# One of four weight-block sums of every turn by seven products moves from VectorE to an adding transfer on the GpSimd queue

## The chip, the cores and the metric

The kernel runs on one core of a Trainium2 chip. The metric is the device time of one execution in microseconds (us), lower is better; three runs of the kernel before are given. A profile is one further execution, recorded by the hardware profiler.

## What is computed

Two transformer-like blocks over 256 tokens and 2048 features, all in float32. The first is a gated MLP with a spatial mixing, the second holds attention, an mLSTM and a gated convolutional MLP. Nearly all of the arithmetic is in products of the 256 tokens with large weight matrices:

```python
z = h @ w_in                                  # (256 x 2048) @ (2048 x 12288): u, v, gate
x = x + (y * jax.nn.silu(gate)) @ w_out       # (256 x 4096) @ (4096 x 2048)        phase out1
z = jnp.einsum('bsd,de->bse', h, w_in[l])     # 2048 -> 10256                        vv, side, gm
x = x + jnp.einsum('bsd,de->bse', merged, w_out[l])                               #  out2
u = causal_dwconv(jnp.einsum('bsd,df->bsf', h2, w_up[l]), conv_w[l], conv_b[l])   #  up
x = x + jnp.einsum('bsf,fd->bsd', jax.nn.silu(u_gate) * u_val, w_down[l])         #  down
```

## The kernel before

**The stream of weights.** All weights lie in HBM as chunks of 128 partitions x 1024 float32 (512 KB, 256 rows by 512 columns of a matrix), in the order in which they are used. Every weight is used once. TensorE multiplies in a reduced float32 format (`fp32r`), so each chunk is split in two: ScalarE copies it into `w_hi` in that format (`high_of_chunk`, line 1014, "hi" below), VectorE computes `w_lo` = chunk - `w_hi` (`low_of_chunk`, line 1432, "lo" below), and TensorE makes three matmuls of every tile: hi by hi, lo by hi and hi by lo. `w_hi` and `w_lo` are rings of four slots. ScalarE starts the hi of item n once TensorE is through with item n - 4 (`mm_done`), VectorE follows (`hi_ready`), and TensorE waits for `lo_ready`. Every engine takes its work in one fixed order, that of the list `ITEMS`.

**Items.** An ordinary item is one chunk of the stream (12 matmuls, 16 in phase up). In the phases v, out1, gm0, gm1, out2 and down some of the work is done in *turns by seven products*: a turn there covers a 2 x 2 set of matrix blocks B11, B12, B22, B21 (each a chunk of its own, with a buffer of its own), and the eight block products of the two token tiles and two column halves are made out of seven, by sums of row tiles and sums of weight blocks (the Winograd form of Strassen's scheme). A product is an item of 6 matmuls. There are 21 such turns (`QUADS`): 5 in v, 4 in out1, 3 in gm0 and gm1, 2 in out2, 7 in down. Their products stand between the chunks C0 to C3 of an ordinary turn; "a chunk item" is one of those:

```python
MIXED = (1, "C0", 5, 7, "C1", 6, 3, "C2", 4, 2, "C3")
MIXED_LATE = ("C0", 1, "C1", 5, 7, "C2", 6, 3, "C3", 4, 2)      # gm1 and out2
```

**The sums of weight blocks.** Product 1 multiplies B11, product 3 B22, product 2 B21. The other four multiply sums, which VectorE makes in place (`block_sum`, line 1437), called *T1* to *T4* here in the order in which they are made: T1 = B12 - B11 (into B11's buffer, for product 5), T3 = B22 - B12 (into B12's buffer, for product 7), T2 = B22 - T1 (for product 6), T4 = B21 - T2 (for product 4). T1 is made after the lo of product 1, T3 after the lo of the item behind product 1, T2 after the lo of product 5. ScalarE's hi of product 7 waits for T3 by the semaphore `block_sums`.

**Queues.** All weights are loaded by SyncE's queue (`raw` chunks four ahead into a ring, line 504, and the blocks, line 491), each after the lo of the item that used its buffer. GpSimd (POOL) has 14 small operations (`rstd`, line 2042, a power) and nothing else.

**Order of back-to-back turns.** In `WIDE_STEPS` a pair such as `(2, 4)` is one turn by products mixed with one ordinary turn. Of the 21 turns by products 9 follow directly on another of them in the same phase, in `MIXED` order; 9 stand in `MIXED` order behind ordinary chunk items; 3 are in `MIXED_LATE` order.

```python
"down": (((3, None), (4, None), (8, None), (9, None), (5, 0), (6, 1), (7, 2), (10, None)),
         ((3, 0), (7, None), (4, 1), (5, 2), (8, 6), (9, None), (10, None))),
```

Of the kernel before, what the change touches and what calls it, by code (L numbers as in the profile page):

```python
# [13 lines left out]
M_HEADS = 4  # L14
# [161 lines left out]
def quad_of(item):  # L176

    return QUADS.index((item.phase, item.group, item.turn))
# [84 lines left out]
def build(nc, x, x_tokens, stream, w_s, params, gain_rows, final_rows, gate_w, identity, consts, out):  # L263
# [208 lines left out]
    with block:  # L472
# [520 lines left out]
        def _(act):  # L993
# [3 lines left out]
            def high_of_chunk(n):  # L997

                item = ITEMS[n]
                if item.product:  # L1000
                    b, uses = PRODUCT_OF[item.product], quad_of(item)
                    of = wide[item.phase].blocks[buffer_of(uses, b)]
                    if item.product in (1, 3, 2):
                        act.wait_ge(block_full[b], 16 * (uses + 1))
                    else:
                        act.wait_ge(sem["block_sums"], 4 * uses + {5: 1, 7: 2, 6: 3, 4: 4}[item.product])
                else:
                    c = CHUNK_COUNT[n]
                    of = raw[:, c % RING, :]
                    act.wait_ge(raw_full[c % RING], 16 * (c // RING + 1))  # L1010
                if n >= RING:

                    act.wait_ge(mm_done, n - RING + 1)
                activation(w_hi[:, n % RING, :], of[:], ACT.Copy).then_inc(hi_ready, 1)  # L1014
# [405 lines left out]
        def _(dve):  # L1420
# [13 lines left out]

            def block_sum(item, to, a, b):
                to, a, b = (wide[item.phase].blocks[buffer_of(quad_of(item), k)] for k in (to, a, b))
                v.tensor_tensor(to[:], a[:], b[:], ALU.subtract).then_inc(sem["block_sums"], 1)

            def block_sums(n):

                item, before = ITEMS[n], ITEMS[n - 1]
                if item.product == 1:
                    uses = quad_of(item) + 1
                    dve.wait_ge(block_full[B11], 16 * uses)
                    dve.wait_ge(block_full[B12], 16 * uses)
                    dve.wait_ge(lo_ready, n + 1)
                    block_sum(item, B11, B12, B11)
                elif before.product == 1:
                    uses = quad_of(before) + 1
                    dve.wait_ge(block_full[B22], 16 * uses)  # L1450
                    dve.wait_ge(sem["block_sums"], 4 * uses - 3)
                    block_sum(before, B12, B22, B12)
                elif item.product == 5:
                    dve.wait_ge(lo_ready, n + 1)
                    block_sum(item, B11, B22, B11)
                elif item.product == 6:
                    dve.wait_ge(block_full[B21], 16 * (quad_of(item) + 1))
                    dve.wait_ge(lo_ready, n + 1)
                    block_sum(item, B11, B21, B11)
# [53 lines left out]
            def sums_of_rows(phase, n, a_hi, a_lo):  # L1513

                if n in SUMS_AT[phase]:
                    i = SUMS_AT[phase].index(n)
                    at_i = slice(4 * SUM_TURNS[phase][i], 4 * SUM_TURNS[phase][i] + 4)
                    rows, sums = wide[phase].rows, wide[phase].sums
                    link(v.tensor_tensor(rows[:], a_hi[:, at_i, :].bitcast(F32), a_lo[:, at_i, :].bitcast(F32), ALU.add))
                    a11, a21 = rows[:, 0:2, 0:P], rows[:, 0:2, P:S]  # L1520
                    a12, a22 = rows[:, 2:4, 0:P], rows[:, 2:4, P:S]
                    v.tensor_tensor(sums[:, 2], a11, a21, ALU.subtract)
                    link(v.tensor_tensor(sums[:, 0], a21, a22, ALU.add))
                    link(v.tensor_tensor(sums[:, 1], sums[:, 0], a11, ALU.subtract))
                    v.tensor_tensor(sums[:, 3], a12, sums[:, 1], ALU.subtract).then_inc(sem["sums_ready"], 1)

            def sums_low(phase, n):
# [5 lines left out]
            def own_products(phase, n):  # L1533


                p1, u_a, u_b = wide[phase].p1, wide[phase].u_a, wide[phase].u_b
                for name, g in GROUPS_BY_PRODUCTS:
                    if name != phase:
                        continue
                    after = n - product_item(phase, g, last_by_products(phase, g), 6)  # L1540
                    if after == 0:
                        dve.wait_ge(sem["p1_ready"], own_ahead(phase, g) + 1)
                        dve.wait_ge(mm_done, n + 1)
                        link(v.tensor_tensor(u_a[:], XS[:, 2, :], p1[:], ALU.add))
                    if after == 2:
                        link(v.tensor_tensor(u_b[:], XS[:, 3, :], u_a[:], ALU.add))
                    if after == 4:
                        link(v.tensor_tensor(u_a[:], XS[:, 1, :], u_a[:], ALU.add))
# [8 lines left out]
            def v_result(q):  # L1557

                half = q % 2
                dve.wait_ge(mm_done, half_end("v", q // 2, half) + 1)  # L1560
                to = v_all[:, :, col_block(q)]
                by_t = ((v_wide.p1, v_wide.u_b), (v_wide.u_a, v_wide.u_d))[half]
                for t in range(2):
                    ins = v.tensor_tensor(to[:, t, :], GG[:, 2 * half + t, :], by_t[t][:], ALU.add)  # L1564
                ins.then_inc(group_read[half], 1)

            for n in range(items_of("v")):
# [92 lines left out]
            def add_products(phase, n, to):  # L1660

                p1, u_a, u_b = wide[phase].p1, wide[phase].u_a, wide[phase].u_b
                for g in range(2):
                    n0, n1 = col_block(2 * g), col_block(2 * g + 1)
                    at_6 = product_item(phase, g, last_by_products(phase, g), 6)
                    after = n - at_6
                    if after == 0:
                        dve.wait_ge(sem["p1_ready"], own_ahead(phase, g) + 1)
                        dve.wait_ge(mm_done, at_6 + 1)
                        link(v.tensor_tensor(u_a[:], XS[:, 2, :], p1[:], ALU.add))  # L1670
                        v.tensor_tensor(to[:, 0, n0], to[:, 0, n0], p1[:], ALU.add)
                    if after == 1:
                        link(v.tensor_tensor(u_b[:], XS[:, 3, :], u_a[:], ALU.add))
                        v.tensor_tensor(to[:, 1, n0], to[:, 1, n0], u_b[:], ALU.add)
                    if after == 2:
                        link(v.tensor_tensor(u_a[:], XS[:, 1, :], u_a[:], ALU.add))
                        v.tensor_tensor(to[:, 0, n1], to[:, 0, n1], u_a[:], ALU.add)
                    if after == 3:
                        link(v.tensor_tensor(u_b[:], XS[:, 1, :], u_b[:], ALU.add))
                        link(v.tensor_tensor(to[:, 1, n1], to[:, 1, n1], u_b[:], ALU.add))  # L1680
                        dve.sem_inc(sem["own_read"], 1)

            out1_second = product_item("out1", 1, 4, 1) - FIRST_ITEM["out1"] - 8
# [184 lines left out]
            def gate_m_result(gm, h):  # L1868

                dve.wait_ge(mm_done, half_end(gm, 0, h) + 1)  # L1870
                by_t = ((gm_wide.p1, gm_wide.u_b), (gm_wide.u_a, gm_wide.u_d))[h]
                for t in range(2):
                    ins = v.tensor_tensor(gate_m[h][:, t, :], GG[:, 2 * h + t, :], by_t[t][:], ALU.add)
                ins.then_inc(group_read[h], 1)

            def a_projected(p, h):
# [159 lines left out]
        @block.gpsimd  # L2036
        def _(pool):
            p = nc.gpsimd

            def rstd(to, of, count, value, after):  # L2040
                pool.wait_ge(sem[count], value)
                p.tensor_tensor(to, of, minus_half[:, 0:of.shape[1]], ALU.pow).then_inc(sem[after], 1)

            pool.wait_ge(sem["minus_half_ready"], 1)
            rstd(n_rstd[:, 0:2], n_ms[:, 0:2], "ms_ready", 1, "rstd_ready")
            rstd(v_stat[:, 4:6], v_stat[:, 2:4], "v_ms_ready", 1, "v_rstd_ready")
            rstd(n_rstd[:, 0:2], n_ms[:, 0:2], "ms_ready", 2, "rstd_ready")
            rstd(n_rstd[:, 2:4], n_ms[:, 2:4], "ms_ready", 3, "rstd_ready")
            for n in range(4):
                rstd(q_rstd[:], q_ms[:], "q_ms_ready", n + 1, "q_rstd_ready")  # L2050
            for m in range(M_HEADS):
                rstd(m_rstd[:], m_ms[:], "m_ms_ready", m + 1, "m_rstd_ready")
            rstd(n_rstd[:, 0:2], n_ms[:, 0:2], "ms_ready", 4, "rstd_ready")


def chunks_of(w):
# [75 lines left out]
```

## Time and profile before

| | |
|---|---|
| time, median of 3 runs | 2098.22 us (2098.14 to 2098.47) |
| profiled execution, span | 2095.9 us |
| TensorE (PE) busy | 2089.8 us, 100% of the span, 10000 matmuls |
| VectorE (DVE) busy | 1506.6 us, 72% |
| ScalarE (ACT) busy | 1112.4 us, 53% |
| GpSimd (POOL) busy | 17.5 us, 1% |
| DMA queue of SyncE | 394.66 MB, 57.1% of the 16 DMA engines' span |

The time of a run stands 2.3 us above the span of the profiled execution. Times in the views are microseconds from the span's start. Matmuls are pipelined, so that one is recorded as 0.39 us long although the next starts 0.23 us after it.

### The profile page before, as it was taken

How to read it: one execution, taken by the hardware profiler on the slowest of the kernel's cores; microseconds unless marked ns; L12 is line 12 of the kernel's file. 1: busy time of each engine (PE TensorE's matmuls, PEld its weight loads, DVE VectorE, ACT ScalarE, POOL GpSimd, SP SyncE). 2: the span in 40 equal slices, each digit the busy share in tenths (PEclk: the TensorE clock that was granted, in tenths of full speed). 3: DMA queues.
4: the chain of work that ended last, by engine and by line, in shares of the span. 5: the costliest groups of instructions: out<-in, count | busy, mean ns of one | idle time of the engine just before them, and what ended most of it. 6: DMA issues, size and time to landing. Idle time of an engine off the chain costs nothing.

```text
span 2095.9 us, 25218 instructions
## 1 busy us (share of the span) xinstructions
PE 2089.8 (100%) x10000; PEld 1750.1 (84%) x10000; DVE 1506.6 (72%) x1702; ACT 1112.4 (53%) x1314; POOL 17.5 (1%) x17
## 2 busy tenths in 40 slices
PE   9999999999999999999999999999999999999999
PEld 7888888888888887888888888888888888888887
DVE  7987656655787754665669678867777777779986
ACT  6765444444456544555455454555555555555553
POOL 0000000000000000100000000000000000000000
PEclk9999999999999999999999999999999999999999
DMA  8665555555764555544465656556556566556663
GB/s 337 210 200 175 198 187 187 194 187 189 272 214 157 194 194 171 177 155 153 150 210 181 221 169 208 167 185 192 187 185 195 183 192 190 181 181 232 224 203 133
DMA packets 111957, 404.40 MB, mean 193 GB/s; under 512 B 12512, under 2 KB 13280, under 8 KB 111328
## 3 DMA queue, kind: packets, MB, share of 16 engines
q1 hardware_dynamic: 109440, 394.66, 57.1%
q10 hardware_dynamic: 2400, 8.14, 1.0%
q8 instruction: 79, 1.29, 0.3%
q14 instruction: 38, 0.31, 0.0%
HBM read 400.65 MB, written 2.10 MB: 192 GB/s over the span
## 4 chain that ended last, share of the span: by engine, by line
PE 96%; DVE 3%; ACT 1%; DMA 0%; issue 0%; ACTq 0%; DVEq 0%
PE g L556 37%; PE g L653 23%; PE xs L581 8%; PE g L581 8%; PE xs L676 5%; PE xs L585 4%; PE g L585 4%; PE g L680 4%; DVE w_lo L1432 1%; PE xs L604 1%; PE xs L713 1%; ACT w_hi L1014 0%; PE xs L833 0%; DMA xf<-in_x 0%; PE xs L830 0%
## 5 line engine op out<-in xcount | busy, mean ns | idle before, releaser
L1432 DVE TENSOR_TENSOR w_lo<-raw,w_hi 128x1024 fp32r<-128x1024 f32 x659 | 803.4, 1223 | 492.6 <-ACT w_hi L1014 486.9
L1014 ACT ACTIVATE w_hi<-raw 128x1024 fp32r<-128x1024 f32 x659 | 697.4, 1059 | 756.6 <-PE g L556 411.7
L556 PE MATMUL g<-w_hi,mid_both 128*128 128x512 f32 x1024 | 326.7, 394 | 0.0
L556 PE MATMUL g<-w_hi,in_both 128*128 128x512 f32 x1024 | 318.8, 390 | 0.1
L556 PEld LDWEIGHTS g<-w_hi,in_both 128*128 128x128 f32 x1024 | 192.2, 188 | 40.3 <-DVE v_all L1564 0.5
L556 PEld LDWEIGHTS g<-w_hi,mid_both 128*128 128x128 f32 x1024 | 192.3, 188 | 39.6
L556 PE MATMUL g<-w_lo,mid_both 128*128 128x512 f32 x512 | 199.4, 389 | 0.0
L556 PE MATMUL g<-w_lo,in_both 128*128 128x512 f32 x512 | 199.2, 389 | 0.0
L581 PE MATMUL g<-mlp_both,w_hi 128*128 128x512 f32 x704 | 176.8, 393 | 0.0
L581 PE MATMUL xs<-mlp_both,w_hi 128*128 128x512 f32 x704 | 176.3, 392 | 0.0
L581 PEld LDWEIGHTS g<-mlp_both,w_hi 128*128 128x128 f32 x704 | 126.5, 189 | 22.8
L581 PEld LDWEIGHTS xs<-mlp_both,w_hi 128*128 128x128 f32 x704 | 126.6, 189 | 22.6
L653 PE MATMUL g<-w_hi,in_both 128*128 128x512 f32 x352 | 112.6, 390 | 1.3 <-DVE w_lo L1500 1.0
L556 PEld LDWEIGHTS g<-w_lo,in_both 128*128 128x128 f32 x512 | 96.1, 188 | 19.7
L556 PEld LDWEIGHTS g<-w_lo,mid_both 128*128 128x128 f32 x512 | 96.3, 188 | 19.1
L585 PEld LDWEIGHTS g<-mlp_both,w_lo 128*128 128x128 f32 x704 | 96.2, 190 | 7.0
L585 PEld LDWEIGHTS xs<-mlp_both,w_lo 128*128 128x128 f32 x704 | 96.0, 190 | 6.9
L585 PE MATMUL g<-mlp_both,w_lo 128*128 128x256 f32 x704 | 98.3, 282 | 0.0
L585 PE MATMUL xs<-mlp_both,w_lo 128*128 128x256 f32 x704 | 98.2, 282 | 0.0
L653 PE MATMUL g<-w_hi,f_hi 128*128 128x512 f32 x240 | 93.7, 390 | 0.2
L653 PE MATMUL g<-w_hi,f_lo 128*128 128x512 f32 x240 | 93.4, 389 | 0.0
L653 PE MATMUL g<-w_lo,f_hi 128*128 128x512 f32 x240 | 93.4, 389 | 0.0
(404 smaller groups left out, 3044.3 us busy)
## 6 DMA issues: line engine op xcount, KB each, us to landing
raw<-in_stream SPq DMA_DIRECT2D x659, 512.0 KB, 3.5
d_block<-in_stream SPq DMA_DIRECT2D x28, 512.0 KB, 4.6
o_block<-in_stream SPq DMA_DIRECT2D x24, 512.0 KB, 4.7
v_block<-in_stream SPq DMA_DIRECT2D x20, 512.0 KB, 4.4
gm_block<-in_stream SPq DMA_DIRECT2D x12, 512.0 KB, 5.1
x_first<-in_x_tokens ACTq DMA_DIRECT2D x2, 1024.0 KB, 6.8
gain_row<-in_gain_rows SPq DMA_DIRECT2D x8, 256.0 KB, 3.5
xt<-in_x_tokens ACTq DMA_DIRECT2D x1, 2048.0 KB, 8.0
```

What stands on the lines that cost most here:

```text
L556: ins = mm(G[buf][:, t, :], a[:, kt, at_t], w[:, slot, j * COLS:(j + 1) * COLS], start=(kt == 0 and n == 0), stop=(last and j == ROWS_PER_ ...
L581: mm(UP[buf][:, b, :, :], w_hi[:, slot, j * COLS + b * P:j * COLS + (b + 1) * P], a_both[:, :, kt, :], start=(kt == 0), stop=False, skip_g ...
L585: ins = mm(UP[buf][:, b, 0, :], w_lo[:, slot, j * COLS + b * P:j * COLS + (b + 1) * P], a_both[:, 0, kt, :], start=False, stop=(last and j ...
L604: ins = turn(TR[:, b, t * P:(t + 1) * P], of[:, t, b * P:(b + 1) * P], ident[:])
L653: ins = mm(GG[:, bank, :], a[:, kt, t * P:(t + 1) * P], w[:, slot, half_chunk(j)], start=n == 0 and opens(item, bank), stop=ended and n == ...
L676: ins = mm(XS[:, own[p], :], a, w[:, slot, half_chunk(j)], start=first and opens_own(item), stop=last and j == 1 and n == 2, skip_group_ch ...
L680: ins = mm(GG[:, RESULT_OF[p], :], a, w[:, slot, half_chunk(j)], start=first and opens(item, RESULT_OF[p]), stop=False, skip_group_check=True)
L713: ins = mm(SV[:, t, :], w[:, t, :], a[:, t, :], start=(n == 0), stop=(n == 2))
L1014: activation(w_hi[:, n % RING, :], of[:], ACT.Copy).then_inc(hi_ready, 1)
L1432: v.tensor_tensor(w_lo[:, n % RING, :], of, w_hi[:, n % RING, :].bitcast(F32), ALU.subtract).then_inc(lo_ready, 1)
```

## The change

T3 is no longer made on VectorE. GpSimd's queue issues a transfer, `add_block`, once per turn by products: it reads the chunk of B22 from HBM a second time and adds it to what lies in B12's buffer (`accum_op=ALU.add`). It waits for T1 (`block_sums` at 3q + 1 for the turn number q), because T1 reads the same buffer; ScalarE's hi of product 7 waits for its end (`block_added`). Since the transfer can only add, the signs of some blocks and of the sums of rows are turned: T1 = B12 + B11, T3 = B12 + B22, T2 = T1 + B22, T4 = T2 + B21, and the results of the second column half are subtracted where they were added. The `rstd` operations of GpSimd keep their order and are put between the transfers.

```diff
@@ high_of_chunk, ScalarE @@
                     if item.product in (1, 3, 2):
                         act.wait_ge(block_full[b], 16 * (uses + 1))
+                    elif item.product == 7:
+                        act.wait_ge(sem["block_added"], 16 * (uses + 1))
                     else:
-                        act.wait_ge(sem["block_sums"], 4 * uses + {5: 1, 7: 2, 6: 3, 4: 4}[item.product])
+                        act.wait_ge(sem["block_sums"], 3 * uses + {5: 1, 6: 2, 4: 3}[item.product])
@@ block_sum and block_sums, VectorE @@
             def block_sum(item, to, a, b):
                 to, a, b = (wide[item.phase].blocks[buffer_of(quad_of(item), k)] for k in (to, a, b))
-                v.tensor_tensor(to[:], a[:], b[:], ALU.subtract).then_inc(sem["block_sums"], 1)
+                v.tensor_tensor(to[:], a[:], b[:], ALU.add).then_inc(sem["block_sums"], 1)
 
             def block_sums(n):
 
-                item, before = ITEMS[n], ITEMS[n - 1]
+                item = ITEMS[n]
                 if item.product == 1:
                     uses = quad_of(item) + 1
                     dve.wait_ge(block_full[B11], 16 * uses)
                     dve.wait_ge(block_full[B12], 16 * uses)
                     dve.wait_ge(lo_ready, n + 1)
                     block_sum(item, B11, B12, B11)
-                elif before.product == 1:
-                    uses = quad_of(before) + 1
-                    dve.wait_ge(block_full[B22], 16 * uses)
-                    dve.wait_ge(sem["block_sums"], 4 * uses - 3)
-                    block_sum(before, B12, B22, B12)
                 elif item.product == 5:
+                    dve.wait_ge(block_full[B22], 16 * (quad_of(item) + 1))
                     dve.wait_ge(lo_ready, n + 1)
                     block_sum(item, B11, B22, B11)
@@ sums_of_rows, VectorE @@
                     v.tensor_tensor(sums[:, 2], a11, a21, ALU.subtract)
-                    link(v.tensor_tensor(sums[:, 0], a21, a22, ALU.add))
-                    link(v.tensor_tensor(sums[:, 1], sums[:, 0], a11, ALU.subtract))
+                    link(v.tensor_tensor(sums[:, 0], a22, a21, ALU.subtract))
+                    link(v.tensor_tensor(sums[:, 1], sums[:, 0], a11, ALU.add))
                     v.tensor_tensor(sums[:, 3], a12, sums[:, 1], ALU.subtract).then_inc(sem["sums_ready"], 1)
@@ add_products, VectorE (the same kind of edit in own_products, v_result, gate_m_result) @@
                     if after == 2:
                         link(v.tensor_tensor(u_a[:], XS[:, 1, :], u_a[:], ALU.add))
-                        v.tensor_tensor(to[:, 0, n1], to[:, 0, n1], u_a[:], ALU.add)
+                        v.tensor_tensor(to[:, 0, n1], to[:, 0, n1], u_a[:], ALU.subtract)
@@ GpSimd @@
+            def add_block(n):
+
+                item = ITEMS[n]
+                if item.product == 1:
+                    q = quad_of(item)
+                    pool.wait_ge(sem["block_sums"], 3 * q + 1)
+                    p.dma_start(wide[item.phase].blocks[buffer_of(q, B12)][:],
+                                stream[chunk_in_stream(item.phase, item.group, 1, 2 * item.turn + 1)],
+                                accum_op=ALU.add).then_inc(sem["block_added"], 16)
+
             pool.wait_ge(sem["minus_half_ready"], 1)
-            rstd(n_rstd[:, 0:2], n_ms[:, 0:2], "ms_ready", 1, "rstd_ready")
-            rstd(v_stat[:, 4:6], v_stat[:, 2:4], "v_ms_ready", 1, "v_rstd_ready")
-            rstd(n_rstd[:, 0:2], n_ms[:, 0:2], "ms_ready", 2, "rstd_ready")
-            rstd(n_rstd[:, 2:4], n_ms[:, 2:4], "ms_ready", 3, "rstd_ready")
-            for n in range(4):
-                rstd(q_rstd[:], q_ms[:], "q_ms_ready", n + 1, "q_rstd_ready")
-            for m in range(M_HEADS):
-                rstd(m_rstd[:], m_ms[:], "m_ms_ready", m + 1, "m_rstd_ready")
-            rstd(n_rstd[:, 0:2], n_ms[:, 0:2], "ms_ready", 4, "rstd_ready")
+            for n in range(1, FIRST_ITEM["end"]):
+                add_block(n)
+                if n == FIRST_ITEM["v"] + 18:
...
+                if n == FIRST_ITEM["up"]:
+                    rstd(n_rstd[:, 0:2], n_ms[:, 0:2], "ms_ready", 4, "rstd_ready")
```

VectorE in the second turn by products of phase down, before. `d_block_166` holds B11, `d_block_167` B12 and `d_block_165` B22:

```order
L1432 TENSOR_TENSOR w_lo<-d_block_166,w_hi 128x1024
L1437 TENSOR_TENSOR d_block_166<-d_block_167,d_block_166 128x1024
L1432 TENSOR_TENSOR w_lo<-raw,w_hi 128x1024
L1437 TENSOR_TENSOR d_block_167<-d_block_165,d_block_167 128x1024
L1432 TENSOR_TENSOR w_lo<-d_block_166,w_hi 128x1024
L1437 TENSOR_TENSOR d_block_166<-d_block_165,d_block_166 128x1024
L1432 TENSOR_TENSOR w_lo<-d_block_167,w_hi 128x1024
```

The same place after the change:

```order
L1434 TENSOR_TENSOR w_lo<-d_block_166,w_hi 128x1024
L1439 TENSOR_TENSOR d_block_166<-d_block_167,d_block_166 128x1024
L1434 TENSOR_TENSOR w_lo<-raw,w_hi 128x1024
L1434 TENSOR_TENSOR w_lo<-d_block_166,w_hi 128x1024
L1439 TENSOR_TENSOR d_block_166<-d_block_165,d_block_166 128x1024
L1434 TENSOR_TENSOR w_lo<-d_block_167,w_hi 128x1024
```

The fourth of the seven operations, T3, is gone, and all others keep their order.

ScalarE at the same place, with the semaphores that each instruction waits for, before:

```order
L1014 ACTIVATE w_hi<-d_block_166 128x1024 [waits mm_done,block_full0]
L1014 ACTIVATE w_hi<-raw 128x1024 [waits mm_done,raw_full0]
L1014 ACTIVATE w_hi<-d_block_166 128x1024 [waits mm_done,block_sums]
L1014 ACTIVATE w_hi<-d_block_167 128x1024 [waits mm_done,block_sums]
L1014 ACTIVATE w_hi<-raw 128x1024 [waits mm_done,raw_full1]
```

and after the change:

```order
L1016 ACTIVATE w_hi<-d_block_166 128x1024 [waits mm_done,block_full0]
L1016 ACTIVATE w_hi<-raw 128x1024 [waits mm_done,raw_full0]
L1016 ACTIVATE w_hi<-d_block_166 128x1024 [waits mm_done,block_sums]
L1016 ACTIVATE w_hi<-d_block_167 128x1024 [waits mm_done,block_added]
L1016 ACTIVATE w_hi<-raw 128x1024 [waits mm_done,raw_full1]
```

Nothing moved on ScalarE; the hi of product 7 (the fourth row) waits for the transfer. On TensorE the order of instructions is the same in both kernels.

## Rows read from the trace of the kernel before

**Rows 1.** The page, part 1: busy time, share, instructions of each engine.

```profile
PE 2089.8 (100%) x10000; PEld 1750.1 (84%) x10000; DVE 1506.6 (72%) x1702; ACT 1112.4 (53%) x1314; POOL 17.5 (1%) x17
```

**Rows 2.** Waits of TensorE over the whole span: in total, times, longest (us).

```profile
PE xs L609 <- DVE ones L1487: 1.1, 1, 1.1
PE g L653 <- DVE w_lo L1500: 1.0, 1, 1.0
PE g L653 <- DVE v_all L1564: 0.2, 1, 0.2
PE xs L780 <- DVE gw_both L1474: 0.2, 1, 0.2
```

**Rows 3.** The page, part 4: shares of the chain that ended last.

```profile
PE 96%; DVE 3%; ACT 1%; DMA 0%; issue 0%; ACTq 0%; DVEq 0%
```

**Rows 4.** Groups by line: the sums of blocks in down (xcount | busy us, mean ns).

```profile
L1437 DVE TENSOR_TENSOR d_block<-d_block,d_block 128x1024 f32<-128x1024 f32 x28 | 34.3, 1224 | 2.3 <-DVE w_lo L1432 0.5
```

**Rows 5.** Timeline of VectorE, second turn by products of down (start, us).

```profile
1922.20 1.23 DVE L1432 TENSOR_TENSOR w_lo<-d_block,w_hi 128x1024 fp32r<-128x1024 f32 x1 [1.49 <-ACT w_hi L1014]
1923.56 1.23 DVE L1437 TENSOR_TENSOR d_block<-d_block,d_block 128x1024 f32<-128x1024 f32 x1
1924.70 1.22 DVE L1432 TENSOR_TENSOR w_lo<-raw,w_hi 128x1024 fp32r<-128x1024 f32 x1
1925.84 1.22 DVE L1437 TENSOR_TENSOR d_block<-d_block,d_block 128x1024 f32<-128x1024 f32 x1
1926.97 1.22 DVE L1432 TENSOR_TENSOR w_lo<-d_block,w_hi 128x1024 fp32r<-128x1024 f32 x1
1928.23 1.23 DVE L1437 TENSOR_TENSOR d_block<-d_block,d_block 128x1024 f32<-128x1024 f32 x1
1929.37 1.22 DVE L1432 TENSOR_TENSOR w_lo<-d_block,w_hi 128x1024 fp32r<-128x1024 f32 x1
```

**Rows 6.** Timeline of ScalarE in the same stretch: hi of products 5 and 7.

```profile
1924.82 1.06 ACT L1014 ACTIVATE w_hi<-d_block 128x1024 fp32r<-128x1024 f32 x1 [1.29 <-DVE d_block L1437]
1927.09 1.06 ACT L1014 ACTIVATE w_hi<-d_block 128x1024 fp32r<-128x1024 f32 x1 [1.21 <-DVE d_block L1437]
```

**Rows 7.** Timeline of TensorE: first and last of the six matmuls of that product 7.

```profile
1931.73 0.39 PE L676 MATMUL xs<-w_hi,d_sums_hi 128*128 128x512 f32 x1
...
1932.87 0.39 PE L676 MATMUL xs<-w_hi,d_sums_lo 128*128 128x512 f32 x1
```

**Rows 8.** Timelines: T1 of the first turn in v, then its product 7.

```profile
48.02 1.23 DVE L1437 TENSOR_TENSOR v_block<-v_block,v_block 128x1024 f32<-128x1024 f32 x1
...
57.42 0.39 PE L676 MATMUL xs<-w_hi,v_sums_hi 128*128 128x512 f32 x1
```

**Rows 9.** Timelines: T1 of the fourth turn of down, then its product 7.

```profile
1972.64 1.23 DVE L1437 TENSOR_TENSOR d_block<-d_block,d_block 128x1024 f32<-128x1024 f32 x1
...
1983.41 0.39 PE L676 MATMUL xs<-w_hi,d_sums_hi 128*128 128x512 f32 x1
```

**Rows 10.** SyncE's DMA queue, issues (KB each, median us to landing), all blocks' landing.

```profile
q1 hardware_dynamic: 109440, 394.66, 57.1%
...
raw<-in_stream SPq DMA_DIRECT2D x659, 512.0 KB, 3.5
...
x_first<-in_x_tokens ACTq DMA_DIRECT2D x2, 1024.0 KB, 6.8
...
final_row<-in_final_rows ACTq DMA_DIRECT2D x1, 1024.0 KB, 12.1
...
DMA to landing us min/median/max: 3.0/4.7/9.4
```

**Rows 11.** Timeline: a wait of GpSimd for VectorE, and the operation before it.

```profile
55.16 0.16 DVE L1485 TENSOR_SCALAR n_ms<-n_sum 128x2 f32<-128x2 f32 x1
...
55.47 1.53 POOL L2042 TENSOR_TENSOR n_rstd<-n_ms,minus_half 128x2 f32<-128x2 f32 x1 [55.03 <-DVE n_ms L1485]
```

**Rows 12.** Timeline of SyncE's queue in the turn of rows 5.

```profile
1920.74 5.54 SPq L504 DMA_DIRECT2D raw<-in_stream  x2
```

More of the change, by code:

```diff
@@ L1543, in own_products @@
                         dve.wait_ge(mm_done, n + 1)
-                        link(v.tensor_tensor(u_a[:], XS[:, 2, :], p1[:], ALU.add))
+                        link(v.tensor_tensor(u_a[:], p1[:], XS[:, 2, :], ALU.subtract))
                     if after == 2:
@@ L1563, in v_result @@
                 for t in range(2):
-                    ins = v.tensor_tensor(to[:, t, :], GG[:, 2 * half + t, :], by_t[t][:], ALU.add)
+                    ins = v.tensor_tensor(to[:, t, :], GG[:, 2 * half + t, :], by_t[t][:], ALU.subtract if half else ALU.add)
                 ins.then_inc(group_read[half], 1)
@@ L1669, in add_products @@
                         dve.wait_ge(mm_done, at_6 + 1)
-                        link(v.tensor_tensor(u_a[:], XS[:, 2, :], p1[:], ALU.add))
+                        link(v.tensor_tensor(u_a[:], p1[:], XS[:, 2, :], ALU.subtract))
                         v.tensor_tensor(to[:, 0, n0], to[:, 0, n0], p1[:], ALU.add)
@@ L1676, in add_products @@
                         link(v.tensor_tensor(u_a[:], XS[:, 1, :], u_a[:], ALU.add))
-                        v.tensor_tensor(to[:, 0, n1], to[:, 0, n1], u_a[:], ALU.add)
+                        v.tensor_tensor(to[:, 0, n1], to[:, 0, n1], u_a[:], ALU.subtract)
                     if after == 3:
                         link(v.tensor_tensor(u_b[:], XS[:, 1, :], u_b[:], ALU.add))
-                        link(v.tensor_tensor(to[:, 1, n1], to[:, 1, n1], u_b[:], ALU.add))
+                        link(v.tensor_tensor(to[:, 1, n1], to[:, 1, n1], u_b[:], ALU.subtract))
                         dve.sem_inc(sem["own_read"], 1)
@@ L1872, in gate_m_result @@
                 for t in range(2):
-                    ins = v.tensor_tensor(gate_m[h][:, t, :], GG[:, 2 * h + t, :], by_t[t][:], ALU.add)
+                    ins = v.tensor_tensor(gate_m[h][:, t, :], GG[:, 2 * h + t, :], by_t[t][:], ALU.subtract if h else ALU.add)
                 ins.then_inc(group_read[h], 1)
@@ L2042, in rstd @@
                 p.tensor_tensor(to, of, minus_half[:, 0:of.shape[1]], ALU.pow).then_inc(sem[after], 1)
-            pool.wait_ge(sem["minus_half_ready"], 1)
-            rstd(n_rstd[:, 0:2], n_ms[:, 0:2], "ms_ready", 1, "rstd_ready")
-            rstd(v_stat[:, 4:6], v_stat[:, 2:4], "v_ms_ready", 1, "v_rstd_ready")
-            rstd(n_rstd[:, 0:2], n_ms[:, 0:2], "ms_ready", 2, "rstd_ready")
-            rstd(n_rstd[:, 2:4], n_ms[:, 2:4], "ms_ready", 3, "rstd_ready")
-            for n in range(4):
-                rstd(q_rstd[:], q_ms[:], "q_ms_ready", n + 1, "q_rstd_ready")
-            for m in range(M_HEADS):
-                rstd(m_rstd[:], m_ms[:], "m_ms_ready", m + 1, "m_rstd_ready")
-            rstd(n_rstd[:, 0:2], n_ms[:, 0:2], "ms_ready", 4, "rstd_ready")
+            def add_block(n):
[6 more added lines that the diff above has]
+                                accum_op=ALU.add).then_inc(sem["block_added"], 16)
+            pool.wait_ge(sem["minus_half_ready"], 1)
+            for n in range(1, FIRST_ITEM["end"]):
+                add_block(n)
+                if n == FIRST_ITEM["v"] + 18:
+                    rstd(n_rstd[:, 0:2], n_ms[:, 0:2], "ms_ready", 1, "rstd_ready")
+                if n == FIRST_ITEM["ug"]:
+                    rstd(v_stat[:, 4:6], v_stat[:, 2:4], "v_ms_ready", 1, "v_rstd_ready")
+                if n == FIRST_ITEM["vv"]:
+                    rstd(n_rstd[:, 0:2], n_ms[:, 0:2], "ms_ready", 2, "rstd_ready")
+                    rstd(n_rstd[:, 2:4], n_ms[:, 2:4], "ms_ready", 3, "rstd_ready")
+                if n == FIRST_ITEM["side"]:
+                    for k in range(4):
+                        rstd(q_rstd[:], q_ms[:], "q_ms_ready", k + 1, "q_rstd_ready")
+                    for m in range(M_HEADS):
+                        rstd(m_rstd[:], m_ms[:], "m_ms_ready", m + 1, "m_rstd_ready")
+                if n == FIRST_ITEM["up"]:
+                    rstd(n_rstd[:, 0:2], n_ms[:, 0:2], "ms_ready", 4, "rstd_ready")
 def chunks_of(w):
```

## The prediction

> **What bounds the kernel now.** I read the page first. TensorE is busy for 2089.8 of the 2095.9 us of the span [rows 1], and the chain that ended last runs through it for 96% [rows 3]. A matmul's recorded end is modelled, so a busy share alone could hide idle time; I therefore looked at TensorE's waits. There are four, 2.5 us in all, two of them before the first item [rows 2]. So in the steady state TensorE always finds its next operands. VectorE, at 72%, works ahead of it. What can change the time is only whether something comes to be late for TensorE.
>
> How far the others are ahead I read from the timeline of one turn by products in down, the second there. VectorE's lo of product 1 starts at 1922.20, T1 at 1923.56, so T1 ends at 1924.79; then come lo of the chunk, T3, lo of product 5, T2, and lo of product 7 from 1929.37 to 1930.59 [rows 5]. ScalarE waits for T1 before the hi of product 5 and for T3 before that of product 7 [rows 6]. TensorE starts product 7 at 1931.73 [rows 7]: lo of product 7 was there 1.14 us early. The reader is to see that T3 is a short link (ScalarE started 0.02 us after its end at 1927.07), and that the whole lead of the ring at this place is about one microsecond plus what VectorE would gain by a shorter list.
>
> **What it removes.** One of four sums in each of 21 turns. A sum takes 1224 ns [rows 4], so VectorE has 21 x 1.22 = 25.7 us less to do. None of it is on the path: TensorE waits for VectorE for 2.5 us in all, at places without a sum of blocks [rows 2]. The gain to the end is taken as 0 and can't be above 2.5 us. The row sums and the results keep their number of operations; only their signs change: 0. The wait for B22 goes from T3 to T2, one item later, which can only help.
>
> **What it adds.** In each turn, a chain in place of T3: T1 ends, GpSimd sees it and issues the transfer, the transfer reads B22 from HBM and adds it to B12's buffer, ScalarE sees its end and makes the hi of product 7. Queued behind that instruction on ScalarE are the hi of the chunk C1, of product 6 and so on, since ScalarE keeps its order; VectorE's lo of product 7 and all behind it wait for them, and TensorE waits for that lo.
>
> *How long may it take?* In the turn of rows 5 TensorE wants product 7 at 1931.73, its first weight load one matmul step (0.23 us) sooner, at 1931.50. Back from there: lo 1.22, hi 1.06, and about 0.15 for the two handings over, makes 2.43: ScalarE has to start by 1929.07, which is 4.3 us after the end of T1 [rows 5 to 7]. VectorE's own work doesn't come in between any more (lo of the chunk, lo of product 5 and T2 are three steps of 1.14 to 1.26, done by 1928.4). The 4.3 us hold for the 9 turns that follow directly on another one: the items ahead are then small, products 4 and 2 of the last turn among them. I count the first turn of gm0 with them, since VectorE comes to it late out of phase side: 10 turns. In the fourth turn of down, behind ordinary chunks, T1 ends at 1973.87 and product 7 starts at 1983.41 [rows 9]: less 0.23 and 2.43 that leaves 6.9. In the first turn of v it is 49.25 to 57.42 [rows 8], which leaves 5.5. By their timelines 4 turns lie between 5.5 and 6.9, and 7 (three of them in the late order) at 6.9 to 8.
>
> *How long does it take?* The trace has no transfer from GpSimd's queue and none that adds. Bounds: it can't be quicker than the quickest block load of the same 512 KB, 3.0 us, and for the other end I take the slowest 1024 KB load, 12.1 [rows 10]. An adding transfer has 512 KB to read in HBM and the 512 KB to which it adds; that is nearest to a load of 1024 KB, 6.8 us in this trace with the stream running beside it [rows 10]. It won't have the engines to itself here either: SyncE issues two raw loads in this stretch, the second when T3 used to start [rows 12]. GpSimd's start after VectorE's semaphore is 0.15 us (55.32 to 55.47) [rows 11]. I take 6.8 + 0.1 = 6.9 us from the end of T1 to the start of hi.
>
> *The sum.* TensorE's wait in a turn is what 6.9 goes beyond its allowance. Ten turns: 10 x (6.9 - 4.3) = 26. Four turns between: 1.4 in the first, half of that on average, 3. Seven turns: 0. Together 29 us of new waiting. I don't let one turn's wait spill into the next: after a late product 7, VectorE has the lo of 8 items and T4 to do, 9 x 1.14 = 10.3 us, while TensorE has 3 chunk items and 5 products, 3 x 2.72 + 5 x 1.36 = 15.0 us by its step of 0.23 (five steps from 1931.73 to 1932.87, so 1.36 for the six matmuls of a product and twice that for a chunk's twelve) [rows 7], so the lead is rebuilt before the next T1. Profiled execution: 2095.9 + 29 = 2125; the median of the runs stands 2.3 us above the span, so 2127.
>
> **A rule against this sum.** No row shows GpSimd's queue. The Trainium skill, "DMA: Bandwidth & Descriptors", section on the anatomy of one DMA, gives a GpSimd-issued transfer as about 2.0 us plus its bytes over 436 GB/s, which would be 3.2 us for 512 KB. "Collectives: The Full Stack", on the fold count, says that the adding costs nothing by itself but needs two reads, so counted as twice the bytes it would be 4.4 us. By that estimate nearly every turn would stay within its allowance, and the time would be about 2100; no run here shows it yet.
>
> **Rivals.**
> 1. *The transfer lands in time, no change.* Mechanism: the whole link takes under 4.7 us. Ten waits of up to 0.4 are then 4 us. For it: plain loads of this size land in 3.5 median, block loads in 4.7 [rows 10], and with the second read hidden under the first the link would be like one of them. Against: that is the price without adding and without GpSimd's issue, and the allowance is already used up by it. At 4.3 or less the time is 2098, at 4.7 it is 2102.
> 2. *The transfer is much slower*, as the 12.1 us row: then no turn is spared. The allowances add up to about 10 x 4.3 + 4 x 6.1 + 7 x 7.5 = 120 us, 21 x 12.1 = 254, so 134 us of waiting: 2232. It needs engines held up by the stream; they are at 57.1%, and only one load of this size was so late [rows 10]. From 9.4 (the slowest block load) on: 21 x 9.4 - 120 = 77 us, 2175.
> 3. *Faster.* VectorE's 25.7 us would have to come through to TensorE. The waits that they could shorten are 2.5 us long in all [rows 2], so it can be no more than 2096 even with a timely transfer. More would need matmuls that step faster when VectorE does less, of which nothing is seen: within a product they step evenly [rows 7].
>
> **How the numbers follow.** A measurement of this kernel can tell about 0.2%, 4 us, from no change. Forecast (link of 4.7 to 9.4 us, slower): 0.72, likeliest 2127. In time: 0.19. Slower than 9.4: 0.06. Faster: 0.03. So slower 0.78, same 0.19, faster 0.03. The range begins at no wait at all, 2098, and ends at a link of about 8.5 us: 10 x 4.2 + 4 x 2.4 + 7 x 1.2 = 60 us, 2158; I close it at 2160.
>
> **What would show it.** In the profile after: VectorE 25 us less busy, 63 sums of blocks in place of 84; a GpSimd queue with 21 transfers of 512 KB and a time to landing, forecast near 6.8; ScalarE's waits for a DMA into a block, about 21 x 4.6 us long less its waits for TensorE; and new waits of TensorE for `w_lo`, none at other places, 2 to 3 us each in the turns that follow on another one and none behind ordinary chunks. If landing is under 4.5 us, the likeliest case is wrong and nothing waits. If TensorE waits longer than the landing says, the lead isn't rebuilt as I say. If its waits are at raw chunks, the transfer has held up the stream.

## The result and the profile after

The changed kernel takes 2122.39 us (median of 4 runs, 2119.61 to 2124.24) against 2098.18 us before: a ratio of 1.0114, 95% interval 1.01 to 1.0129, 24.2 us slower. The profiled execution has a span of 2117.8 us, 21.9 more than that of before; it is the quickest of the four runs.

The page after: the span, part 1, GpSimd's queue in part 3 (packets, MB, share of the 16 engines' span) and the chain that ended last.

```profile
span 2117.8 us, 25218 instructions
...
PE 2093.6 (99%) x10000; PEld 1749.9 (83%) x10000; DVE 1483.4 (70%) x1681; ACT 1109.0 (52%) x1314; POOL 35.2 (2%) x38
...
q0 software_dynamic: 3024, 11.01, 3.1%
...
PE 87%; DVE 5%; DMA 4%; ACT 2%; issue 2%; ACTq 0%; DVEq 0%; POOL 0%; POOLq 0%
```

Beside [rows 1]: VectorE has 23.2 us less to do, and TensorE, which issues what it issued, is in the span 21.9 us longer. DMA, with 0% in [rows 3], is now 4% of the chain. TensorE's waits (in total, times, longest, us), which answer to [rows 2] (two more, of 0.2 us each, are as before):

```profile
PE xs L676 <- DVE w_lo L1434: 17.9, 12, 2.6
PE xs L609 <- DVE ones L1485: 1.1, 1, 1.1
PE g L653 <- DVE w_lo L1498: 0.8, 1, 0.8
PE g L653 <- DVE w_lo L1434: 0.4, 1, 0.4
```

The first row is new: 12 waits for the lo of a product. The recorded waits are 17.9 us; from the start of one matmul to the start of the next, less the step of 0.227, the gaps at these and at the fourth row add up to 20.4 us. ScalarE's waits for a transfer into a block are one for each of the 21 turns and 80.0 us in all; of down and gm:

```profile
ACT w_hi L1016 <- DMA d_block<-in_stream: 32.0, 7, 6.8
...
ACT w_hi L1016 <- DMA gm_block<-in_stream: 12.4, 3, 5.4
```

The turn that [rows 5 to 7] show stands here after the change. VectorE (T1 at 1938.96, T2 at 1942.65):

```profile
1938.96 1.23 DVE L1439 TENSOR_TENSOR d_block<-d_block,d_block 128x1024 f32<-128x1024 f32 x1
1940.11 1.22 DVE L1434 TENSOR_TENSOR w_lo<-raw,w_hi 128x1024 fp32r<-128x1024 f32 x1
1941.32 1.23 DVE L1434 TENSOR_TENSOR w_lo<-d_block,w_hi 128x1024 fp32r<-128x1024 f32 x1
1942.65 1.23 DVE L1439 TENSOR_TENSOR d_block<-d_block,d_block 128x1024 f32<-128x1024 f32 x1
1947.56 1.22 DVE L1434 TENSOR_TENSOR w_lo<-d_block,w_hi 128x1024 fp32r<-128x1024 f32 x1 [3.68 <-ACT w_hi L1016]
```

GpSimd's queue, ScalarE's hi of product 7, and TensorE from the last matmul of product 5 to the first of product 7:

```profile
1940.49 0.86 POOL L2048 DMA_DIRECT2D d_block<-in_stream  x1 [23.22 <-DVE d_block L1439]
```

```profile
1946.46 1.06 ACT L1016 ACTIVATE w_hi<-d_block 128x1024 fp32r<-128x1024 f32 x1 [5.18 <-DMA d_block<-in_stream]
```

```profile
1946.90 0.39 PE L676 MATMUL xs<-w_hi,d_sums_lo 128*128 128x512 f32 x1
1948.83 0.50 PE L676 MATMUL xs<-w_hi,d_sums_hi 128*128 128x512 f32 x1 [1.54 <-DVE w_lo L1434]
```

T1 ends at 1940.19. GpSimd issues the transfer 0.30 us later, ScalarE starts its hi at 1946.46: the link took 6.27 us where T3 had let it start after 2.30. VectorE had everything else done at 1943.88 and stood still for 3.7 us. TensorE, which had product 7's operands 1.14 us early before, starts it 1.93 us after product 5's last matmul, 1.70 us late. The transfer itself: the issue of the seven in down (duration min/median/max in ns), and the landing of all 21 (min/median/max in us):

```profile
L2048 POOL DMA_DIRECT2D d_block<-in_stream x7: 862/865/902, 1916.4 to 2069.6; - x7
...
DMA to landing us min/median/max: 5.3/5.8/7.8
```

### The profile page after: what moved, and what is told of

It reads as the page before. It is cut to its first block, busy times and chain, and to the rows that moved or that the text cites. A ratio compares the mean times of both kernels' runs of the same rounds, so it can differ in the third digit from the quotient of the medians.

```text
span 2117.8 us, 25218 instructions
## 1 busy us (share of the span) xinstructions
PE 2093.6 (99%) x10000; PEld 1749.9 (83%) x10000; DVE 1483.4 (70%) x1681; ACT 1109.0 (52%) x1314; POOL 35.2 (2%) x38
## 3 DMA queue, kind: packets, MB, share of 16 engines
q0 software_dynamic: 3024, 11.01, 3.1%
## 4 chain that ended last, share of the span: by engine, by line
PE 87%; DVE 5%; DMA 4%; ACT 2%; issue 2%; ACTq 0%; DVEq 0%; POOL 0%; POOLq 0%
PE g L556 36%; PE g L653 18%; PE xs L581 8%; PE g L581 8%; PE xs L585 4%; PE g L585 4%; PE xs L676 4%; DVE w_lo L1434 3%; PE g L680 2%; ACT w_hi L1016 2%; DMA d_block<-in_stream 1%; PE xs L604 1%; DMA v_block<-in_stream 1%; DMA raw<-in_stream 1%; DMA gm_block<-in_stream 1%
```

## The experiments

All kernels were timed against the kernel before on the same chip, 2097.97 to 2098.06 us there. The ratios are to it. The diffs show the lines that matter; the counts of the semaphores that follow from them are left out.

**Where the transfer stands, and what VectorE's time is worth.** Four kernels. First (e1), the changed kernel with the chunk C1 ahead of product 7:

```diff
-MIXED = (1, "C0", 5, 7, "C1", 6, 3, "C2", 4, 2, "C3")
+MIXED = (1, "C0", 5, "C1", 7, 6, 3, "C2", 4, 2, "C3")
```

> The changed kernel with the chunk item C1 put ahead of product 7 in the MIXED order (18 of 21 turns), so that TensorE wants product 7 one chunk item, 2.7 us, later. Theory A (each turn costs what the link from T1 to hi of product 7, 6.1 us in the profile after, exceeds its allowance of about 4.6 us, and nothing else): the allowance becomes 7.3 us in the turns that follow on another one, the waits of TensorE for product 7 vanish, 2098 to 2100 us. Rival B (the adding transfer costs by its traffic or by GpSimd beside VectorE, wherever it stands): the time stays at 2110 or more, with waits at other places. Rival C (VectorE's 25 us bring something once the waits are gone): below 2095.

Second (e2), the same edit of the kernel before, as its control:

> The kernel before with the same new order of MIXED, T3 still on VectorE: the control for e1. Theory A: TensorE is never waited for at either place, so 2098 us as before, within 1 us. Rival: the order itself is worth or costs something (VectorE has T3 in the way of the chunk's lo, banks of PSUM opened earlier), 2 us or more either way; then e1 has to be read against this one and not against the kernel before.

Third (e3), the kernel before without T3:

```diff
-                elif before.product == 1:
-                    uses = quad_of(before) + 1
-                    dve.wait_ge(block_full[B22], 16 * uses)
-                    dve.wait_ge(sem["block_sums"], 4 * uses - 3)
-                    block_sum(before, B12, B22, B12)
```

> The kernel before with T3 left out altogether (product 7 multiplies B12 as it was loaded, no transfer added): it shows what the 21 sums, 25.7 us of VectorE, are worth by themselves. Theory A: nothing, 2098 us within 1 us, since TensorE waits for VectorE for 2.5 us in all. Rival C: the freed VectorE time shows, 2095 or less.

Fourth (e4), the transfer only in nine turns with a large allowance:

```diff
+def by_transfer(q):
+    return q not in (0, 1, 4, 6, 8, 9, 10, 14, 15, 16, 19, 20)
...
+                elif before.product == 1 and not by_transfer(quad_of(before)):
+                    uses = quad_of(before) + 1
+                    dve.wait_ge(block_full[B22], 16 * uses)
+                    dve.wait_ge(sem["block_sums"], sums_before(uses - 1) + 1)
+                    block_sum(before, B12, B22, B12)
```

> The changed kernel with the adding transfer in the 9 turns alone in which the profile after shows no wait for product 7 (allowance 6.9 us or more), T3 back on VectorE in the other 12. Theory A: no wait, 2098 to 2099 us. Rival B (each transfer costs something wherever it stands, about 24 us over 21 of them = 1.15 us each): 2108 us.

Measured:

| kernel | median us | ratio (95%) |
|---|---|---|
| e1: transfer, C1 ahead of product 7 | 2100.91 | 1.0015 (1.0006 to 1.0024) |
| e2: before, C1 ahead of product 7 | 2098.78 | 1.0004 (0.9996 to 1.0013) |
| e3: before without T3 | 2097.45 | 0.9997 (0.9989 to 1.0006) |
| e4: transfer in nine turns | 2099.24 | 1.0005 (0.9996 to 1.0014) |

With all 21 transfers in place, one exchange in the order takes back 21.5 of the 24.3 us. So the transfers cost by where their end is wanted, and neither by traffic nor by GpSimd beside VectorE: rival B falls. TensorE's waits that are left in the first kernel for `w_lo`:

```profile
PE g L680 <- DVE w_lo L1434: 0.9, 2, 0.5
PE xs L676 <- DVE w_lo L1434: 0.6, 1, 0.6
```

The control has waits for `w_lo` too:

```profile
PE g L653 <- DVE w_lo L1500: 0.4, 1, 0.4
PE g L653 <- DVE w_lo L1432: 0.4, 2, 0.2
```

So the 1.5 us here against 0.8 us there make 0.7 us of the 1.8 us between the two profiled runs (2098.4 and 2096.6 us); the rest I can't place, and the time is 0.9 us above what I had said. The first and the fourth kernel hold all the other edits of the change, the turned signs among them, so these cost at most the 2.9 and 1.2 us by which the two are slower. VectorE's 25.7 us are worth nothing that can be told from no change (third row), so a version of this idea has at most 0.6 us to gain. None of my versions beats the kernel before.

**The tight turns alone.** The same function with the other choice (e5):

```diff
+def by_transfer(q):
+    return q in (1, 4, 6, 8, 9, 10, 15, 16, 19, 20)
```

> The counterpart of e4: the adding transfer in the 10 turns alone that I had called tight (nine that follow directly on another one, and the first of gm0), T3 on VectorE in the other 11. Theory A: the waits of those turns in the profile after add up to 17.5 us of 20.4, so 2115 to 2120 us. Rival B (1.15 us for every transfer): 2110 us.

Measured: 2121.22 us, 1.0112 (1.0098 to 1.0125). Ten transfers cost nearly what 21 do, where nine others cost 1.2 us. The price is above my 2115 to 2120 us: the waits are 18.0 us, but one is 4.80 us long, and behind it TensorE ran slower (last section). That wait is of the second turn of v, which has the smallest allowance of all (3.84 us in the kernel before). Its transfer was issued at 72.02 and landed only 8.5 us later, against 6.3 us in the same turn of the changed kernel:

```profile
80.50 1.06 ACT L1027 ACTIVATE w_hi<-v_block 128x1024 fp32r<-128x1024 f32 x1 [7.70 <-DMA v_block<-in_stream]
```

Why this one landed so late was not tested.

**What the link is made of.** A plain copy from the same queue, nothing added (e6):

```diff
-                                stream[chunk_in_stream(item.phase, item.group, 1, 2 * item.turn + 1)],
-                                accum_op=ALU.add).then_inc(sem["block_added"], 16)
+                                stream[chunk_in_stream(item.phase, item.group, 1, 2 * item.turn + 1)]).then_inc(sem["block_added"], 16)
```

> The changed kernel with the transfer as a plain copy from the same queue: B22 is written over B12 and nothing is added. It measures what the adding is in the link. If the second read costs as I predicted (a load of 1024 KB against one of 512 KB, 6.8 against 3.5), landing falls from 5.8 to about 3.5 plus GpSimd's issue, 4.5 us, the link to 4.8, and the time to 2098 plus about 4 = 2102 us. Rival (the adding costs next to nothing, the queue sets the link): landing stays at 5.5 or more, 2119 us or more.

The same copy from SyncE's queue, and none from GpSimd's (e7):

```diff
+                if n and ITEMS[n - 1].product == 1:
+                    q, of = quad_of(ITEMS[n - 1]), ITEMS[n - 1]
+                    sp.wait_ge(sem["block_sums"], 3 * q + 1)
+                    sp.dma_start(wide[of.phase].blocks[buffer_of(q, B12)][:],
+                                 stream[chunk_in_stream(of.phase, of.group, 1, 2 * of.turn + 1)]).then_inc(
+                        sem["block_added"], 16)
```

> As e6, but the plain copy is issued by SyncE's queue, which waits for T1 at its place in the order. It measures GpSimd's issue (0.86 us long, and a start 0.30 us after T1's end). If the queue is a small part: landing as other block loads, 4.5 us, link 4.7, waits of 0 to 0.4 us in ten turns, 2098 to 2102 us. If it is most of the link: 2098 here and 2115 or more in e6.

Adding, but from B22's buffer and not from HBM (e8):

```diff
-                                stream[chunk_in_stream(item.phase, item.group, 1, 2 * item.turn + 1)],
+                                wide[item.phase].blocks[buffer_of(q, B22)][:],
```

> The changed kernel with the adding transfer reading B22 from its buffer on the chip and not a second time from HBM; it waits for B22's load too. Result as before. If the HBM read and its contention with the stream make the landing long: landing falls below 5 us and the time to 2105 or less. If the adding or the queue does: landing stays at 5.3 or more, 2117 us or more.

Measured: plain copy by GpSimd 2098.91 us, 1.0007 (0.9998 to 1.0016); by SyncE 2098.23 us, 1.0001 (0.9993 to 1.001); adding from the buffer 2122.5 us, 1.0116 (1.0102 to 1.013). The plain copy by GpSimd, its issue and its landing, and its queue on the page:

```profile
L2048 POOL DMA_DIRECT2D d_block<-in_stream x7: 527/530/568, 1904.2 to 2049.7; - x7
...
DMA to landing us min/median/max: 3.5/3.8/5.5
```

```profile
q0 software_dynamic: 3024, 11.01, 1.6%
```

Against 5.8 us landing and 3.1% for the adding one: 2.0 us less in landing, 0.33 us of it in the issue (530 against 865 ns), and half the time on the engines (1.6% of 2096.3 us is 1.6 us for each of 21 transfers, 3.1% of 2117.8 us is 3.1 us). My forecast of 3.5 + 1 us for the plain copy was 0.7 too high, and the time that I had put on it (about 2102 us) 3 us. The copy by SyncE, in the turn shown above: T1, the issue, and the landing of all 21:

```profile
1924.22 1.23 DVE L1445 TENSOR_TENSOR d_block<-d_block,d_block 128x1024 f32<-128x1024 f32 x1
1925.47 0.33 SPq L499 DMA_DIRECT2D d_block<-in_stream  x1
...
DMA to landing us min/median/max: 3.2/3.4/5.2
```

SyncE issues it 0.02 us after T1's end at 1925.45, where GpSimd took 0.30 us, and it lands in 3.4 us, where GpSimd's took 3.8. So GpSimd's queue is dearer by about 0.7 us in the link, and the 6.1 us of the link are about 3.4 for the plain copy, 0.7 for the queue and 2.0 for the adding. The adding transfer from the buffer:

```profile
q0 software_dynamic: 3024, 11.01, 3.3%
...
d_block<-d_block POOLq DMA_DIRECT2D x7, 512.0 KB, 5.8
o_block<-o_block POOLq DMA_DIRECT2D x6, 512.0 KB, 5.6
```

It lands as late as from HBM. So the source is not what counts. Beyond a plain copy by SyncE the adding is the larger part of the link, with 2.0 us, and the queue the smaller. That the adding reads the same bytes once more would fit the doubled time on the engines, but no run shows the second read itself: packets and bytes on the page are the same with and without it (3024, 11.01).

**Twice the link.** The transfer of each turn is made twice, one after the other (e9):

```diff
+                    pool.wait_ge(sem["block_added"], 32 * q + 16)
+                    p.dma_start(wide[item.phase].blocks[buffer_of(q, B12)][:], stream[...],
+                                accum_op=ALU.add).then_inc(sem["block_added"], 16)
```

> The changed kernel with the adding transfer made twice in each turn, the second issued when the first has landed (B22 is added twice): it doubles the suspected link. Theory A (a turn waits for what the link exceeds its own allowance): link 0.3 + 5.8 + 0.1 + 5.8 = 12.0 us; the 21 allowances, read from the kernel before as the time from T1's end to product 7 less 2.37 us, add up to 125 us, so 21 x 12.0 - 125 = 127 us of waiting, 2225 us, and all 21 turns wait; more if TensorE's clock falls after waits as it did once in e5 (3.4 us lost there). Rival (a late turn leaves the next one with less lead, so waits grow more than the link): above 2260. Rival (the ring's lead and VectorE's free time absorb part): below 2200.

Measured: 2265.05 us, 1.0795 (1.0781 to 1.081), 40 us above my sum. TensorE's waits, and the windows' row over the whole span (busy us of PE, PEld, DVE, ACT, POOL with counts, granted clock, DMA share, GB/s):

```profile
PE xs L676 <- DVE w_lo L1434: 117.0, 21, 7.9
```

```profile
0.00:2259.70 2259.70, 2136.35 (x10000) 1778.10 (x10000) 1484.19 (x1681) 1107.26 (x1314) 53.41 (x59) 0.97 0.60 189
```

All 21 turns wait, as said. Their late starts add up to 120 us; with the mean link of 11.7 us that the trace shows, 21 x 11.7 - 125 = 121. So the rule of allowances holds over a doubled link, and the lead is rebuilt even then. The rest is not waiting: TensorE is busy 46.6 us longer than in [rows 1] at the same matmuls, with a mean granted clock of 0.97. That rival ("waits grow more than the link") gave the right size for a wrong reason.

**Smaller pieces.** Half of T3 on VectorE, half by the transfer (e10):

```diff
+                elif before.product == 1:
+                    uses = quad_of(before) + 1
+                    dve.wait_ge(block_full[B22], 16 * uses)
+                    dve.wait_ge(sem["block_sums"], 3 * uses - 2)
+                    b12, b22 = (wide[before.phase].blocks[buffer_of(uses - 1, k)] for k in (B12, B22))
+                    v.tensor_tensor(b12[:, half_chunk(0)], b12[:, half_chunk(0)], b22[:, half_chunk(0)],
+                                    ALU.add).then_inc(sem["half_sums"], 1)
```

> T3 shared: VectorE adds the first 512 columns of each partition, the transfer the other 512 (256 KB). With landing = fixed part + read + read, a plain copy of 512 KB at 3.8 us (e6) and an adding one at 5.8 give 2.0 us for each read of 512 KB and 1.8 fixed, so 3.8 us for the adding half; link 4.2, below the 4.6 allowance of the tight turns: 2098 to 2100 us. Rival (adding has a surcharge of its own of 2 us whatever the size): landing 4.8, link 5.1, 0.5 us in ten turns, 2104 us.

And the whole of T3 by two transfers of 256 KB, issued one behind the other (e11):

```diff
+                    p.dma_start(wide[item.phase].blocks[buffer_of(q, B12)][:, half_chunk(0)], ...,
+                                accum_op=ALU.add).then_inc(sem["block_added"], 16)
+                    p.dma_start(wide[item.phase].blocks[buffer_of(q, B12)][:, half_chunk(1)], ...,
+                                accum_op=ALU.add).then_inc(sem["block_added_2"], 16)
```

> The changed kernel with the adding transfer cut into two of 256 KB, issued one behind the other by GpSimd, T3 not on VectorE. If the bytes that pass set the landing, the second half lands one issue (0.86 us) after it would have, link 6.1 to 6.9 and 2122 to 2133 us. If the halves run beside each other and each one is quick (as e10 should show for one), the link is 0.3 + 0.9 + 3.8 + a bit = 5.2 and the time 2108 us or less.

The half transfer: 2100.24 us, 1.0011 (1.0002 to 1.002), and in down (KB, us to landing):

```profile
d_block<-in_stream POOLq DMA_DIRECT2D x7, 256.0 KB, 4.1
```

4.1 us lies nearer to 3.8 (price by bytes) than to 4.8 (a surcharge of its own), and brings most turns within their allowance: five still start late, by 0.1 to 0.9 us and 1.8 us together, and the time is 0.2 us above what I had said. The two halves: 2157.99 us, 1.0284 (1.0263 to 1.0305), where I had expected at most 2133. The first and the second of them (us to landing), and the issue of the second:

```profile
DMA to landing us min/median/max: 3.8/4.2/8.2
```

```profile
L2052 POOL DMA_DIRECT2D d_block<-in_stream x7: 1217/1217/1221, 1945.6 to 2106.6; - x7
...
DMA to landing us min/median/max: 5.4/7.1/8.8
```

The first lands in 4.2 us, as alone; the second in 7.1, issued about 0.5 us later, and its own issue takes 1.22 us. Together about 7.6 us from the first issue, 1.8 more than in one piece. Neither of my two expectations fits. The late starts at product 7 add up to 45.7 us of the 60.2 us by which the profiled run (2156.1 us) is longer than that of before; in the same run TensorE is busy 16.9 us longer than before at the same matmuls, with falls of its clock (last section). Why two adding transfers beside each other take longer than one of the same bytes I haven't tested.

## Why the prediction was right

**What bounds the kernel, and the gain of 0.** Right. TensorE had no steady wait, and T3 left out altogether is worth 0.6 us, inside the noise.

**What it removes.** VectorE's busy time fell by 23.2 us and not by 25.7. The rows of VectorE's work in [rows 5] are 1.23 us long but start 1.14 us apart, and 21 x 1.14 is 23.9. This changes nothing in the sum.

**The allowance.** Right in kind, small in size: 4.3 us predicted for a turn that follows on another. The turn above waited 1.70 us on a link of 6.27, so its allowance is 4.57. I had taken the first weight load to need its operands a step ahead, and it didn't: lo's end stands 0.05 us ahead of the matmul. Read in the kernel before (from T1's end to product 7, less the 2.37 us that hi and lo take here), the allowance is 4.5 to 4.6 us in eight of the ten tight turns, 3.84 in the second of v and 4.89 in the first of gm0. In all twelve turns that wait, the link less this allowance gives the late start measured, within 0.02 us in eleven and within 0.3 us in the first of v. Behind ordinary chunks, the seven turns that I put at 6.9 to 8 us don't wait, and neither do two of the four that I put between.

**The link.** 6.9 predicted, 6.1 measured in the median. The row of the 1024 KB load (6.8 us, [rows 10]) overstates an adding transfer of 512 KB (5.8); the start of GpSimd took 0.30 us and not the 0.1 that I took (where [rows 11] had shown 0.15). This is the term that was mis-sized most. In the ten tight turns the link was 6.2 us in the mean and the allowance 4.5: 0.7 and 0.2 us better than I had said, 9 us in all.

**The sum.** Ten tight turns: 26 predicted, 17 in the profile. The four between: 3 predicted, 2.9 measured, but by two of them, the first of v (0.6) and the first of down (2.3, where the transfer landed only after 7.8 us, with SyncE loading two raw chunks and the blocks beside it). That the two figures agree is luck: I had spread the waits over all four. The same turn has the slowest transfer in e6 (5.5 us), e7 (5.2), e8 (7.9) and e10 (6.0), so its lateness comes neither with the adding nor with the source nor with the queue; what makes it was not tested. The other seven: 0 and 0. Together with one wait at another place (0.6, the fourth row above) 20.4 us of late starts in a span that grew by 21.9, where I had put 29. Nine of the tight turns start 1.4 to 1.7 us late and only the second of v 2.8, where I had named 2 to 3 us as the sign; and two turns behind ordinary chunks wait, where the sign was none.

**The lead rebuilt.** Right: consecutive tight turns wait alike (1.70, then 1.57 us in down), and e9 shows the same with waits of 7 us.

**What the sum left out.** The median grew by 24.2 us and the profiled run, the quickest, by 21.9. The other three runs of the changed kernel (2121.97 to 2124.24) show a mean granted clock of 0.998 to 0.999, this one 1.000. I hadn't counted a price of the waits beyond their length. It made up a part of what I had overstated in the link, so that the median, 2122.4 us, lies nearer to my 2127 than the terms deserve; this too is luck.

**The rule that spoke against it.** The Trainium skill's fit for a GpSimd transfer ("DMA: Bandwidth & Descriptors", the anatomy of one DMA) gives 3.2 us; e6 shows 3.8. The statement in "Collectives: The Full Stack" (the bandwidth ceiling) that the adding costs by its second read agrees with the doubled time on the engines (1.6 to 3.1 us), but the 4.4 us worked out from both stayed 1.4 us short of the measured landing, and that was the whole question: with a landing of 4.4 us the link would have been 4.7, and by the allowances above the waits some 2 us in all (an estimate from that page's figure).

**A slip in the bound.** The end of the range takes 1.2 us in each of seven turns at a link of 8.5, where the allowance of 7.5 that I used in the second rival leaves 1.0: 1.4 us of the 60, of no weight.

## What to carry to other kernels

An engine at 72% with a busier one beside it can be relieved at no gain; ask what its work is waited for by, and how soon. Work moved to a transfer needs an allowance from its last input to its first use: here 4.6 us before a loss, against 6.1 for adding 512 KB, and one exchanged pair in the order of items would have given it 2.7 us more. Price an adding transfer by twice the time of a plain copy on the DMA engines (3.1 against 1.6 us here) and, at 512 KB, by 2.0 us more to its landing (5.8 against 3.8), whether it reads HBM or a buffer on the chip; and a plain copy by GpSimd's queue by 0.7 us more than one by SyncE's.

## What the hardware showed that was not expected

TensorE's clock fell to its lower level, 1.2 GHz (0.50), behind single waits of a few microseconds in a kernel that is otherwise 100% busy. In e5, around the 4.80 us wait in the second turn of v:

```profile
77.68 0.39 PE L685 MATMUL xs<-w_hi,v_sums_lo 128*128 128x512 f32 x1
82.87 0.80 PE L685 MATMUL xs<-w_hi,v_sums_hi 128*128 128x512 f32 x1 [4.80 <-DVE w_lo L1445]
83.46 0.63 PE L685 MATMUL xs<-w_lo,v_sums_hi 128*128 128x512 f32 x1
...
89.58 0.39 PE L662 MATMUL g<-w_hi,in_both 128*128 128x512 f32 x1
89.81 0.40 PE L685 MATMUL xs<-w_hi,v_sums_hi 128*128 128x512 f32 x1
```

and by windows of 1 us (same columns as above; the granted clock is the third number from the end):

```profile
80.00:81.00 1.00, 0.00 (x0) 0.00 (x0) 0.00 (x0) 0.50 (x1) 0.00 (x0) 1.00 0.00 0
81.00:82.00 1.00, 0.00 (x0) 0.00 (x0) 0.41 (x1) 1.00 (x2) 0.00 (x0) 0.94 0.00 0
82.00:83.00 1.00, 0.13 (x1) 0.13 (x1) 1.00 (x2) 1.00 (x2) 0.00 (x0) 0.50 0.00 0
...
88.00:89.00 1.00, 1.00 (x4) 0.77 (x4) 0.69 (x1) 0.00 (x0) 0.00 (x0) 0.65 0.46 74
```

The reader is to see that the clock is granted in full through most of the wait, falls in its last microsecond, and that the matmuls then start 0.43 us apart and not 0.227, until the level returns between 88 and 89 us. In e8, whose waits are as long as those of the changed kernel (its longest is 2.5 us), the same happened behind a wait of 2.47 us, with the fall just after its end:

```profile
78.62 0.39 PE L676 MATMUL xs<-w_hi,v_sums_lo 128*128 128x512 f32 x1
81.48 0.77 PE L676 MATMUL xs<-w_hi,v_sums_hi 128*128 128x512 f32 x1 [2.47 <-DVE w_lo L1434]
82.05 0.63 PE L676 MATMUL xs<-w_lo,v_sums_hi 128*128 128x512 f32 x1
```

while in the profile of the changed kernel no such fall follows on its longest wait, 2.61 us. By their starts the 17 steps behind the wait in e5 took 2.9 us more than at 0.227, the 10 in e8 1.7 us more. So a wait of this length can cost some 2 to 3 us on top of itself or nothing, and the times of kernels with such waits scatter: 2119.61 to 2124.24 us here, 2097.56 to 2098.81 us before. In e11 the level fell in or behind six of the 16 waits, and in e9 in or behind 19 of the 21. What is left of the longer spans beside the late starts is 14.5 us in e11 (60.2 less 45.7) and 43.4 us in e9 (163.8 less 120.4), so 2.4 and 2.3 us for each fall, if all of it is put down to them. What decides between a fall and none behind waits of 2.5 to 3 us the runs don't show: in e11 the level fell with starts that came 2.65, 2.94 and 3.06 us late, and not with one 3.02 us late.
